# The linear recurrence unit of the odd layer, computed tile by tile beside that layer's input projection

## The chip, the core and the metric

The kernel runs on one core of a Trainium2 chip. The metric is the device time of one execution, in microseconds. Five engines of the core work on their own instruction streams and meet at semaphores: TensorE (PE in the profile; PEld is its weight load), VectorE (DVE), ScalarE (ACT), GpSimd (POOL) and SyncE (SP), which here only issues DMAs.

## What is computed

The reference is a model of two blocks; the first has attention and a mixture of experts, the second has an even and an odd layer. The change lies in the odd layer alone, whose mixer is (cut to what matters):

```
proj = h @ w_in                                  # 1024 tokens, 1024 -> 3072 columns
hq, hf, hi, hg, lx, lg = split(proj)             # six times 512 columns
hc = rms_norm(hgrn2(hq, hf, hi)) * silu(hg)
xc = conv_b + sum_j conv_w[j] * shift(lx, 3 - j) # causal convolution, 4 taps
r  = sigmoid(xc @ w_a + b_a)                     # blocks of 64 channels
ig = sigmoid(xc @ w_x + b_x)
a  = exp(-8 * r * softplus(-lam))
u  = sqrt(1 - a*a) * ig * xc                     # the factor is 1 at the first token
h_t = a_t * h_(t-1) + u_t                        # linear recurrence over the tokens
hl = h * silu(lg)
y  = concat(hc, hl) @ w_out
```

`hgrn2` is the other recurrence, in chunks of tokens and in four heads.

## The kernel before, in words

`second` builds the odd layer out of four stages. A stage (`stage`) owns its buffers and semaphores; at its end the semaphores are cleared and all engines meet at a barrier, so no work of one stage lies beside another's.

1. `project("pg", ...)`, lines 82 to 276, multiplies the normed activations `hT` (kept in SBUF as two parts, HI and LO) by the weights in six chunks of 512 columns. For each chunk SP loads 2 MB of weights into `raw` (two buffers, so the load of chunk g waits until chunk g-2 is split), ACT rounds them to the HI part (`split_hi`, line 193) and DVE forms the LO part (`split_lo`, line 204), eight instructions each. PE makes eight groups of 24 matmuls (`product`, line 78), each group into its own one of eight PSUM banks `acc`. ACT copies the even groups out (line 240), DVE the odd ones (line 276), and ACT issues the store of each group (line 242). ACT and DVE have the split of chunk g+1 in their streams ahead of the copies of chunk g, and `split_hi` of chunk g+1 waits for the last group of chunk g-1. The chunks come in the order q and f of `hgrn2` (stored transposed, `oT`), its value and gate (as rows, `orows`), and then the two of the linear recurrence unit: x and gate (transposed, rows 1024 to 2047 of `oT`). The scratch tensors lie in HBM.
2. `hgrn2`, lines 2416 to 2736, takes 8 units of 4 steps (`schedule`). In `prep` of a unit DVE forms differences of decays, ACT takes the exponentials (`hg_ex`, line 2559) and POOL multiplies (`hg_qk`, `hg_qb`, `hg_kb`, lines 2607 to 2616); `step(G)` is the PE work of one of 32 chunks of 128 tokens with its ACT copies (lines 2576 to 2586) and DVE sums. PE begins a unit once POOL has finished it. The parts of unit n+1's prep are interleaved with the steps of unit n.
3. `rg_lru`, lines 2742 to 2918, is the linear recurrence unit: four tiles of 128 channels by 1024 tokens. SP loads x and the gate of a tile from `oT`; DVE makes the convolution, four passes (2870 and 2873); PE the two gate products (2818); ACT the sigmoids (2827 to 2830), then for all tiles in turn the exponentials (2836), the hyperbolic tangents (2839) and the roots (2842); DVE the products and the scan (2903 to 2918); ACT and POOL write the two parts of the result into tiles 4 to 7 of `hT` (2845, 2805).
4. `mix_out("om", ...)` norms and gates the output of `hgrn2`, turns it into tiles 0 to 3 of `hT` and multiplies `hT` by `w_out` (line 726).

Of the kernel before, what the change touches and what calls it, by code (L numbers as in the profile page):

```python
# [14 lines left out]
P = 128  # L15
D = 1024
S = 1024
# [64 lines left out]
def project(nc, name, hT, nk, chunks, gain=None, also=None):  # L82
# [17 lines left out]
    uses = [[sum(groups(c) > j for c in chunks[:g]) for j in range(groups(ch))] for g, ch in enumerate(chunks)]  # L100
# [5 lines left out]
    kept = [[sum(groups(c) > j and "split" not in c for c in chunks[:g]) for j in range(NT)] for g in range(N + 1)]  # L106
    nst = [[16 * kept[g][j] for j in range(groups(ch))] for g, ch in enumerate(chunks)]
# [14 lines left out]
    with stage(nc) as st:  # L122
        raw = st.sb(name + "_raw", [P, 2, nk, BANK])
        w = st.sb(name + "_w", [P, 2, 2, nk, BANK], F32R)
        obuf = st.sb(name + "_o", [P, NT, BANK])
        cut = any("split" in ch for ch in chunks)
        parts = obuf[:, :, :].rearrange("p (x o a) n -> p x o a n", x=2, o=2).bitcast(F32R)
# [4 lines left out]
        acc = [st.ps(f"{name}_acc{j}", [P, BANK]) for j in range(NT)]  # L132
        gain_in = st.sem(name + "_gain_in")
        raw_in = [st.sem(f"{name}_raw_in{s}") for s in range(2)]
        k_in = [st.sem(f"{name}_k_in{k}") for k in range(nk)] if by_k else None
        hi_ok, lo_ok = st.sem(name + "_hi_ok"), st.sem(name + "_lo_ok")
        mm_done = [st.sem(f"{name}_mm{j}") for j in range(NT)]
        copied = [st.sem(f"{name}_copied{j}") for j in range(NT)]
        stored = [st.sem(f"{name}_stored{j}") for j in range(NT)]

        with nc.Block() as block:
            @block.sync
            def _(sp):
# [4 lines left out]
                for g, ch in enumerate(chunks):  # L148
                    if g >= 2:
                        sp.wait_ge(lo_ok, splits_to[g - 1])  # L150
# [5 lines left out]
                    for dst, src in ch["load"]:  # L156
                        sp.dma_start(raw[:, g % 2, 0:ks[g][1], dst], src).then_inc(raw_in[g % 2], 16)
                    if g == 1 and also:
                        also(sp)

            @block.tensor
            def _(pe):
                for g, ch in enumerate(chunks):
# [17 lines left out]

            def split_hi(act, g):

                n = chunks[g]["width"]
                if loads[g]:
                    act.wait_ge(raw_in[g % 2], 16 * sum(loads[g % 2:g + 1:2]))
# [2552 lines left out]

def rg_lru(nc, xT_in, A, hT):

# [239 lines left out]
```

## Time and profile before

| what | value |
|---|---|
| median of 3 runs | 2874.32 us (2871.42 to 2881.37) |
| the profiled execution's own time | 2867.56 us |
| its span in the trace | 2865.8 us |
| PE busy over the span | 2218.6 us (77%) |
| DVE, ACT, POOL busy | 1339.6, 1022.9, 535.9 us |
| first and last group of matmuls of the projection `pg` start | 2184.8 us, the last matmul 2448.6 us |

The span begins with the first instruction seen and ends with the last; positions below are microseconds from its start. The time of an execution is a little longer than its span. A stage's share is read by its stretch of positions.

### The profile page before, as it was taken

Reading aid. Unit: us, or ns where it says so; the run is one execution under the profiler, and the core shown is the slowest. Engines: PE = TensorE matmul, PEld = TensorE weight load, DVE = VectorE, ACT = ScalarE, POOL = GpSimd, SP = SyncE. Lnnn points to the kernel's source line nnn. Section 1 sums busy time; section 2 is a strip of 40 time slices with the busy share of each in tenths; the row PEclk is TensorE's granted clock in tenths of the full one; section 3 lists DMA queues with packets and bytes.
Section 4 is the critical chain, followed back from the end, with each engine's and each line's share of the span. In section 5 each row is a group of like instructions: output and inputs, shape, how many; then the busy total and the mean of one; then the engine's idle time right before and its main releaser. Section 6 shows DMA issues by size and latency. Waiting matters only on the chain. (4 is left out here: it accounts for less than half of the span.)

```text
span 2865.8 us, 34485 instructions
## 1 busy us (share of the span) xinstructions
PE 2218.6 (77%) x12244; PEld 1825.8 (64%) x12244; DVE 1339.6 (47%) x2217; ACT 1022.9 (36%) x1809; POOL 535.9 (19%) x630
## 2 busy tenths in 40 slices
PE   6996953999787599994399997688397999464248
PEld 5775942899775466663388885577386888354137
DVE  4223833655443666663612203677463211475753
ACT  4223732455331355552411100455242111463431
POOL 0000011522010121231200004334130000464122
PEclk7998976999888699997599998689698999677669
DMA  6647727522244399884533113321444311221043
GB/s 217 187 145 192 218 57 230 157 59 66 64 157 156 148 359 365 348 342 160 229 114 109 50 48 100 79 66 33 156 135 151 107 52 48 81 67 43 35 140 103
DMA packets 225569, 399.16 MB, mean 139 GB/s; under 512 B 99200, under 2 KB 121088, under 8 KB 212752
## 3 DMA queue, kind: packets, MB, share of 16 engines
q1 hardware_dynamic: 174912, 294.73, 32.5%
q10 hardware_dynamic: 40480, 83.64, 8.2%
q0 software_dynamic: 10032, 18.90, 1.7%
q8 instruction: 87, 1.43, 0.2%
q14 instruction: 58, 0.48, 0.1%
HBM read 300.16 MB, written 114.85 MB: 145 GB/s over the span
## 5 line engine op out<-in xcount | busy, mean ns | idle before, releaser
L78 PE MATMUL pe_acc<-pe_w,hT 128*128 128x512 f32 x960 | 219.7, 391 | 8.8 <-DVE pe_w L204 8.7
L78 PEld LDWEIGHTS pe_acc<-pe_w,hT 128*128 128x128 f32 x960 | 180.8, 189 | 47.6 <-DVE pe_w L204 10.0
L78 PE MATMUL ex_gu<-hT,ex_xT 128*128 128x512 f32 x792 | 194.4, 401 | 0.8 <-DVE hT L1966 0.8
L1966 DVE TENSOR_TENSOR hT<-ex_raw,hT 128x2048 fp32r<-128x2048 f32 x66 | 150.9, 2288 | 89.7 <-ACT hT L1937 86.2
L78 PE MATMUL pg_acc<-hT,pg_w 128*128 128x512 f32 x768 | 177.4, 393 | 8.6 <-DVE pg_w L204 8.6
L78 PEld LDWEIGHTS pg_acc<-hT,pg_w 128*128 128x128 f32 x768 | 146.0, 190 | 39.8 <-DVE pg_w L204 9.3
L78 PEld LDWEIGHTS ex_gu<-hT,ex_xT 128*128 128x128 f32 x792 | 147.5, 190 | 34.5 <-DVE hT L1966 1.2
L1937 ACT ACTIVATE hT<-ex_raw 128x2048 fp32r<-128x2048 f32 x66 | 126.1, 1912 | 43.2 <-PEq L47 23.9
L276 DVE COPY pe_o<-pe_acc 128x512 f32<-128x512 f32 x28 | 19.4, 692 | 238.5 <-PE pe_acc L78 238.5
L1255 PE MATMUL ab_op<-ab_v,ab_pT 128*128 128x64 f32 x1024 | 121.3, 272 | 0.0
L1895 PE MATMUL ex_dn<-ex_wd,ex_hT 128*128 128x512 f32 x264 | 118.7, 592 | 0.8 <-ACT ex_hT L1931 0.8
L1255 PEld LDWEIGHTS ab_op<-ab_v,ab_pT 128*128 128x128 f32 x1024 | 119.3, 192 | 0.0
L276 DVE COPY pg_o<-pg_acc 128x512 f32<-128x512 f32 x24 | 16.6, 691 | 205.0 <-PE pg_acc L78 205.0
L1266 DVE TENSOR_REDUCE ab_mx<-ab_s 128x1 f32<-128x1024 f32 x64 | 78.4, 1225 | 72.0 <-PE ab_s L1233 72.0
L2405 POOL TENSOR_TENSOR sb_w<-sb_be,sb_pr 128x128 f32<-128x128 f32 (+3 forms) x64 | 83.8, 1314 | 148.7 <-DVE sb_pr L2384 140.3
L78 PE MATMUL pa_acc<-hT,pa_w 128*128 128x512 f32 (+1 forms) x432 | 100.7, 395 | 8.7 <-DVE pa_w L204 8.7
L2707 PE MATMUL hg_s<-hg_qk 128*64 128x64 f32 x768 | 42.5, 262 | 82.3 <-POOL hg_kb L2616 82.3
L1230 PE MATMUL ab_s<-ab_kh,ab_qs 128*128 128x512 f32 x128 | 56.8, 444 | 54.8 <-DVE ab_krs L1287 54.3
L78 PEld LDWEIGHTS pa_acc<-hT,pa_w 128*128 128x128 f32 (+1 forms) x432 | 80.0, 185 | 29.0 <-DVE pa_w L204 9.1
L2384 DVE TENSOR_TENSOR_SCAN sb_pr<-sb_s,sb_ones 128x128 f32<-128x128 f32 (+3 forms) x64 | 86.5, 1351 | 20.5 <-ACT sb_s L2341 20.1
L2707 PEld LDWEIGHTS hg_s<-hg_qk 128*64 128x64 f32 x768 | 40.9, 173 | 84.4 <-issue 84.4
L240 ACT ACTIVATE pe_o<-pe_acc 128x512 f32<-128x512 f32 x28 | 16.6, 593 | 215.7 <-PE pe_acc L78 215.7
(455 smaller groups left out, 5195.6 us busy)
## 6 DMA issues: line engine op xcount, KB each, us to landing
ex_raw<-in_w_gate SPq DMA_DIRECT2D x33, 1024.0 KB, 7.4
ex_raw<-in_w_up SPq DMA_DIRECT2D x33, 1024.0 KB, 11.6
ex_wd<-in_w_down SPq DMA_DIRECT2D x33, 1024.0 KB, 13.8
pe_raw<-in_even_w_in SPq DMA_DIRECT2D x6, 2048.0 KB, 7.9
pg_raw<-in_odd_w_in SPq DMA_DIRECT2D x5, 2048.0 KB, 8.6
scr_q<-pa_o ACTq DMA_DIRECT2D x32, 256.0 KB, 3.9
scr_k<-pa_o ACTq DMA_DIRECT2D x32, 256.0 KB, 3.6
hT<-scr_k SPq DMA_DIRECT2D x16, 512.0 KB, 6.7
```

The lines of the kernel that those rows point to most:

```text
L78: mm = pe.matmul(out, a(p, k), b(q, k), start=(k == 0 and i == 0), stop=(k == n - 1 and i == 2))
L240: act.activation(obuf[0:m, j, 0:n], acc[j][0:m, 0:n], ACT.Copy).then_inc(copied[j], 1)
L276: dve.tensor_copy(obuf[0:m, j, 0:n], acc[j][0:m, 0:n]).then_inc(copied[j], 1)
L1230: pe.matmul(sps[l % 2][:, cc], qs[:, u, ii], kh[:, u, cc], start=True, stop=False)
L1255: mm = pe.matmul(ops[m % 2][:, 0:DV], pT[:, m % 2, k * P:(k + 1) * P], v[:, u, k, :], start=(k == 0), stop=(k == NT - 1))
L1266: dve.reduce_max(mx[:, l:l + 1], sps[l % 2][:, :], AX.X).then_inc(max_done, 1)
L1895: mm = pe.matmul(dn[:, n * BANK:(n + 1) * BANK], hTs[:, b % 2, k, :], wd[:, b % ND, k * D + n * BANK:k * D + (n + 1) * BANK], start=(k == ...
L1937: act.activation(split(s, HI)[:, :, g, :], raw[:, s % NW, g, :].rearrange("p (k n) -> p k n", k=8), ACT.Copy).then_inc(w_hi, 1)
L1966: dve.tensor_tensor(split(s, LO)[:, :, g, :], raw[:, s % NW, g, :].rearrange("p (k n) -> p k n", k=8), split(s, HI)[:, :, g, :].bitcast(F3 ...
L2384: dve.tensor_tensor_scan(pr[:, l % 2, S - n:S][:, ::-1], sps[l % 2][:, 0:n][:, ::-1], ones[:, 0:n], 1.0, ALU.mult, ALU.mult).then_inc(pr_o ...
L2405: pool.tensor_tensor(w[:, l % 4, 0:n], be[:, l % 4, 0:n], pr[:, l % 2, S - n + 1:S + 1], ALU.mult).then_inc(w_ok, 1)
L2707: pe.matmul(sps[G % 2][b0:b0 + HB, (l - 1) * HB:l * HB], qk[:, n % 2, l, half], qk[:, n % 2, l, half], start=True, stop=True, skip_group_c ...
```

## The change

The stage `rg_lru` goes. Its work is now in a class `Lru`, whose methods are called from inside `project` at fixed places of each engine's stream: tile t is worked on while PE makes chunk t+1. The projection's chunks are put in another order, x and gate of the unit first. `project` gets three arguments: `ring`, the number of PSUM banks and output buffers, taken in turn over all chunks (6 here in place of 8, since the unit needs two banks), `nraw`, the number of weight buffers (1 here in place of 2), and `beside`. The result of the unit goes to a scratch tensor `lrT`; `hgrn2` loads it in one DMA of 2 MB, and splits it there into the two parts in `hT`: ACT one tile in each of steps 12 to 15, POOL all four at its end. The other calls of `project` keep 8 and 2 and have chunks of 8 groups (the last chunk of one has 2), so that their banks are taken as before.

The loop over `chunks` with `sp` is SP's stream, `beside.tensor` stands behind each group of PE, `beside.scalar` behind each store issued by ACT, `beside.vector` behind each (possible) copy of DVE; POOL multiplies the gate by its sigmoid in a stream of its own. In `hgrn2`, `lru.load` is in SP's stream, `lru.hi` in ACT's `step`, `lru.lo` in POOL's stream behind `schedule`. In `Lru.scalar` each step waits for what it reads, and `j` 2 also for the product with the gate of the tile before (`hg_ok`). The diff, cut to its core (`slot(g, j)` stands for `j` wherever a bank, buffer or semaphore is named, and `g % nraw` for `g % 2` with `raw`):

```diff
-def project(nc, name, hT, nk, chunks, gain=None, also=None):
+def project(nc, name, hT, nk, chunks, gain=None, also=None, ring=NT, nraw=2, beside=None):
+    base = [sum(groups(c) for c in chunks[:g]) for g in range(N + 1)]
+    slot = lambda g, j: (base[g] + j) % ring
+    uses = [[(base[g] + j) // ring for j in range(groups(ch))] for g, ch in enumerate(chunks)]
...
+        def landed(eng, g, j):
+            eng.wait_ge(stored[slot(g, j)], nst[g][j] + 16)
+        beside = beside(st, landed) if beside else None
...
                 for g, ch in enumerate(chunks):
-                    if g >= 2:
-                        sp.wait_ge(lo_ok, splits_to[g - 1])
+                    if beside and g >= 2:
+                        beside.sync(sp, g - 2)
+                    if g >= nraw:
+                        sp.wait_ge(lo_ok, splits_to[g - nraw + 1])
...
+                if beside:
+                    for g in range(N - 2, N):
+                        beside.sync(sp, g)
+                    beside.sync_end(sp)
...
                         mm.then_inc(mm_done[u], 1)
+                        if beside:
+                            beside.tensor(pe, g, j)
...
                         act.dma_start(dst(j), obuf[0:m, u, 0:n]).then_inc(stored[u], 16)
+                        if beside:
+                            beside.scalar(act, g, j)
...
                             dve.tensor_copy(obuf[0:m, u, 0:n], acc[u][0:m, 0:n]).then_inc(copied[u], 1)
+                        if beside:
+                            beside.vector(dve, g, j)
...
-def rg_lru(nc, xT_in, A, hT):
...
+class Lru:
+    NTI = 4
...
+    def load_x(self, sp, t):
+        self.landed(sp, 0, 2 * t)
+        self.landed(sp, 0, 2 * t + 1)
+        if t >= 2:
+            sp.wait_ge(self.conv, 4 * (t - 1))
+        sp.dma_start(self.x[:, t % 2, 4:S + 4], self.src[t * P:(t + 1) * P, :]).then_inc(self.x_in[t % 2], 16)
+    def load_gate(self, sp, t):
+        self.landed(sp, 1, 2 * t)
+        self.landed(sp, 1, 2 * t + 1)
+        if t >= 1:
+            sp.wait_ge(self.gs_ok, t)
+        sp.dma_start(self.gt[:, :], self.src[512 + t * P:512 + (t + 1) * P, :]).then_inc(self.g_in, 16)
+    def store(self, sp, t):
+        sp.wait_ge(self.hg_ok, t + 1)
+        sp.dma_start(self.out[t * P:(t + 1) * P, :], self.o[:, :]).then_inc(self.kept, 16)
+    def sync(self, sp, g):
+        if g == 0:
...
+            self.load_x(sp, 0)
+            self.load_x(sp, 1)
+        elif g == 1:
+            self.load_gate(sp, 0)
+            self.load_x(sp, 2)
+        elif g <= self.NTI + 1:
+            if g + 1 < self.NTI:
+                self.load_x(sp, g + 1)
+            if g - 1 < self.NTI:
+                self.load_gate(sp, g - 1)
+            self.store(sp, g - 2)
...
+    def tensor(self, pe, g, j):
+        t = g - 1
+        if not (0 <= t < self.NTI and j in (2, 3)):
+            return
+        h = j - 2
...
+        pe.wait_ge(self.conv, 4 * (t + 1))
+        if t or h:
+            pe.wait_ge(self.r_ok, 2 * t + h)
+            pe.wait_ge(self.ig_ok, 2 * t + h)
+        nn = slice(h * BANK, (h + 1) * BANK)
+        pe.matmul(self.pa[:, :], self.wa[:, t, :], self.xc[:, nn], start=True, stop=True)
+        pe.matmul(self.px[:, :], self.wx[:, t, :], self.xc[:, nn], start=True, stop=True).then_inc(self.mm, 1)
+    def scalar(self, act, g, j):
...
+        if j in (2, 3):
...
+            act.activation(self.r[:, nn], self.pa[:, :], ACT.Sigmoid, bias=self.ba[:, t:t + 1]).then_inc(self.r_ok, 1)
+            act.activation(self.ig[:, nn], self.px[:, :], ACT.Sigmoid, bias=self.bx[:, t:t + 1]).then_inc(self.ig_ok, 1)
+        elif j == 4:
...
+            act.activation(self.sg[:, :], self.gt[:, :], ACT.Sigmoid).then_inc(self.sg_ok, 1)
...
+            act.activation(self.a[:, :], self.r[:, :], ACT.Exp, scale=self.sm[12][:, t:t + 1]).then_inc(self.a_ok, 1)
...
+            act.activation(self.xc[:, :], self.r[:, :], ACT.Tanh, scale=self.sm[11][:, t:t + 1]).then_inc(self.th_ok, 1)
+        elif j == 6:
...
+            act.activation(self.xc[:, :], self.xc[:, :], ACT.Sqrt).then_inc(self.mu_ok, 1)
...
+    def vector(self, dve, g, j):
...
+        if j == 0:
...
+            dve.tensor_scalar(cv, src[0], self.cw[:, t, 0:1], self.cb[:, t:t + 1], ALU.mult, ALU.add).then_inc(self.conv, 1)
+            for i, (o, z) in enumerate(((xc, cv), (cv, xc), (xc, cv)), 1):
...
+        elif j == 4:
+            dve.wait_ge(self.ig_ok, 2 * (t + 1))
...
+        elif j == 5:
+            dve.wait_ge(self.a_ok, t + 1)
+            step(dve.tensor_tensor(cv, self.a[:, :], self.a[:, :], ALU.mult))
+            dve.wait_ge(self.th_ok, t + 1)
...
+        elif j == 6:
+            dve.wait_ge(self.mu_ok, t + 1)
...
+            step(dve.memset(self.xc[:, 0:1], 1.0))
+            step(dve.tensor_tensor(cv, xc, self.ig[:, :], ALU.mult))
+            step(dve.tensor_tensor_scan(self.r[:, :], self.a[:, :], cv, 0.0, ALU.mult, ALU.add))
+        elif j == 7:
+            dve.wait_ge(self.gs_ok, t + 1)
+            if t >= 1:
+                dve.wait_ge(self.kept, 16 * t)
+            dve.tensor_tensor(self.o[:, :], self.r[:, :], self.sg[:, :], ALU.mult).then_inc(self.hg_ok, 1)
...
+class LruParts:
+    def load(self, sp):
+        sp.dma_start(self.hT[:, LO, 4:8, :].bitcast(F32), self.src.rearrange("(t p) s -> p t s", p=P)).then_inc(self.raw_in, 16)
+    def hi(self, act, t):
+        act.wait_ge(self.raw_in, 16)
+        act.activation(self.hT[:, HI, 4 + t, :], self.hT[:, LO, 4 + t, :].bitcast(F32), ACT.Copy).then_inc(self.hi_ok, 1)
+    def lo(self, pool, t):
+        pool.wait_ge(self.hi_ok, t + 1)
+        pool.tensor_tensor(self.hT[:, LO, 4 + t, :], self.hT[:, LO, 4 + t, :].bitcast(F32), self.hT[:, HI, 4 + t, :].bitcast(F32),
+                           ALU.subtract).then_inc(self.lo_ok, 1)
...
                 load_qv(1)
+                lru.load(sp)
...
                         act.activation(ob[:, h % 2, c, :], ops[:, 0:P], ACT.Copy).then_inc(ob_ok, 1)
+                    if 12 <= G < 16:
+                        lru.hi(act, G - 12)
...
                 schedule(lambda G: None, prep)
+                for t in range(4):
+                    lru.lo(pool, t)
...
-    project(nc, "pg", hT, 8, [T_chunk(wo, c, scr["oT"], c) for c in (0, 512)] +
-            [row_chunk(wo, 1024 + c, scr["orows"], c) for c in (0, 512)] +
-            [T_chunk(wo, 2048 + c, scr["oT"], 1024 + c) for c in (0, 512)], gain=[(0, A["pre_norm_w_2"][1])])
-    hgrn2(nc, ident, scr["oT"], scr["orows"], C, scr["hc"])
-    rg_lru(nc, scr["oT"][1024:2048, :], A, hT)
+    project(nc, "pg", hT, 8, [T_chunk(wo, 2048 + c, scr["oT"], 1024 + c) for c in (0, 512)] +
+            [T_chunk(wo, c, scr["oT"], c) for c in (0, 512)] +
+            [row_chunk(wo, 1024 + c, scr["orows"], c) for c in (0, 512)], gain=[(0, A["pre_norm_w_2"][1])], ring=6, nraw=1,
+            beside=lambda st, landed: Lru(nc, st, A, scr["oT"][1024:2048, :], scr["lrT"], landed))
+    hgrn2(nc, ident, scr["oT"], scr["orows"], C, scr["hc"], lambda st: LruParts(st, scr["lrT"], hT))
```

## Rows read from the trace of the kernel before

**Rows 1.** Busy time by stage; columns stand in the first line.
```profile
core 0: us, PE busy (x) PEld busy (x) DVE busy (x) ACT busy (x) POOL busy (x), PEclk, DMA share, GB/s
...
2184.00:2452.00 268.00, 264.23 (x1152) 218.06 (x1152) 49.15 (x72) 43.58 (x71) 0.00 (x0) 0.99 0.25 92
2452.00:2638.00 186.00, 92.58 (x1312) 81.26 (x1312) 117.52 (x261) 100.52 (x207) 106.84 (x131) 0.72 0.21 59
2638.00:2737.00 99.00, 21.21 (x32) 8.10 (x32) 68.59 (x70) 33.19 (x32) 20.81 (x10) 0.60 0.16 45
...
2765.00:2866.00 101.00, 91.64 (x411) 75.45 (x410) 37.38 (x59) 22.54 (x77) 23.73 (x46) 0.96 0.31 99
```

**Rows 2.** Timeline, start us and duration us: end of the recurrence stage.
```profile
2638.20 0.53 POOL L2796 MEMSET lr_wa<- 128x512 f32 x1 [17.17 <-POOLq L47]
...
2733.95 2.34 POOL L2805 TENSOR_TENSOR hT<-lr_hg,hT 128x1024 fp32r<-128x1024 f32 x1 [4.57 <-ACT hT L2845]
2737.17 0.32 SPq L405 DMA_DIRECT2D omf_x<-scr_hc  x1
```

**Rows 3.** Timeline of DVE in the projection, first chunks.
```profile
2220.58 0.69 DVE L276 COPY pg_o<-pg_acc 128x512 f32<-128x512 f32 x1 [10.19 <-PE pg_acc L78]
2231.46 0.69 DVE L276 COPY pg_o<-pg_acc 128x512 f32<-128x512 f32 x1 [10.19 <-PE pg_acc L78]
2233.44 5.39 DVE L204 SCALAR_TENSOR_TENSOR pg_w<-pg_raw,pg_g,pg_w 128x512 fp32r<-128x512 f32 x8 [1.29 <-ACT pg_w L193]
```

**Rows 4.** Timeline of ACT in the projection, beginning of chunk 1.
```profile
2232.62 5.02 ACT L193 ACTIVATE pg_w<-pg_raw,pg_g 128x512 fp32r<-128x512 f32 x8 [6.00 <-DVE pg_o L276]
```

**Rows 5.** Timeline of PE and DVE in the linear recurrence stage.
```profile
2648.03 3.32 DVE L2873 SCALAR_TENSOR_TENSOR lr_xc<-lr_x,lr_cw,lr_cv 128x1024 f32<-128x1024 f32 x1
...
2654.14 3.75 PE L2818 MATMUL lr_pa<-lr_xc,lr_wa 128*128 128x512 f32 x4 [20.88 <-DVE lr_xc L2873]
...
2662.21 1.95 PE L2818 MATMUL lr_pa<-lr_xc,lr_wa 128*128 128x512 f32 x4 [2.26 <-ACT lr_ig L2830]
...
2664.00 1.88 PE L2818 MATMUL lr_px<-lr_xc,lr_wx 128*128 128x512 f32 x4
...
2673.30 0.80 DVE L2870 TENSOR_SCALAR lr_cv<-lr_x,lr_cw,lr_cb 128x1024 f32<-128x1024 f32 x1
...
2676.78 1.28 DVE L2873 SCALAR_TENSOR_TENSOR lr_xc<-lr_x,lr_cw,lr_cv 128x1024 f32<-128x1024 f32 x1
...
2686.30 1.28 ACT L2832 ACT_TABLE_LOAD   x1
2687.59 0.20 ACT L2832 ACTIVATE lr_sm<-lr_sm 128x4 f32<-128x4 f32 x1
...
2708.49 2.29 DVE L2914 TENSOR_TENSOR_SCAN lr_hs<-lr_a,lr_u 128x1024 f32<-128x1024 f32 x1
```

**Rows 6.** Groups of the linear recurrence stage: count, busy us, mean ns, idle before.
```profile
L2805 POOL TENSOR_TENSOR hT<-lr_hg,hT 128x1024 fp32r<-128x1024 f32 x4 | 9.4, 2340 | 44.8 <-ACT hT L2845 44.8
...
L2829 ACT ACTIVATE lr_r<-lr_pa,lr_ba 128x1024 f32<-128x1024 f32 x4 | 4.5, 1115 | 27.1 <-PE lr_px L2818 27.1
...
L2842 ACT ACTIVATE lr_xc<-lr_xc 128x1024 f32<-128x1024 f32 x4 | 4.1, 1053 | 1.7 <-DVE lr_xc L2905 1.5
```

**Rows 7.** DMA issues, KB each and us to landing.
```profile
pg_raw<-in_odd_w_in SPq DMA_DIRECT2D x5, 2048.0 KB, 8.6
```

**Rows 8.** Timeline of ACT in the other recurrence.
```profile
2456.64 1.06 ACT L2535 ACTIVATE hg_k<-hg_f 128x1024 f32<-128x1024 f32 x1 [12.42 <-DMA hg_f<-scr_oT]
...
2549.03 0.28 ACT L2586 ACTIVATE hg_ob<-hg_o 128x128 f32<-128x128 f32 x1 [1.63 <-PE hg_o L2736]
...
2552.59 1.29 ACT L2559 ACTIVATE hg_ex<-hg_df 128x512 f32<-128x512 f32 x2 [1.01 <-DVE hg_df L2653]
```

**Rows 9.** Timeline of POOL at the end of the other recurrence.
```profile
2619.77 1.26 POOL L2616 TENSOR_TENSOR hg_kb<-hg_k,hg_el 128x512 f32<-128x512 f32 x1
```

**Rows 10.** The chain that ended last: start us, duration us.
```profile
2765.64 11.94 PE om_acc L726 x48
```

More of the change, by code:

```diff
@@ L104, in project @@
         loads[0] = 0
-    kept = [[sum(groups(c) > j and "split" not in c for c in chunks[:g]) for j in range(NT)] for g in range(N + 1)]
-    nst = [[16 * kept[g][j] for j in range(groups(ch))] for g, ch in enumerate(chunks)]
+    plain = [(base[g] + j) % ring for g, ch in enumerate(chunks) for j in range(groups(ch)) if "split" not in ch]
+    first = sum(groups(ch) for ch in chunks if "split" in ch)
+    nst = [[16 * plain[:max(0, base[g] + j - first)].count(slot(g, j)) for j in range(groups(ch))] for g, ch in enumerate(chunks)]
     def outs(x):
@@ L185, in split_hi @@
                 if loads[g]:
[L186 removed]
+                    act.wait_ge(raw_in[g % nraw], 16 * sum(loads[g % nraw:g + 1:nraw]))
                 if g >= 2:
                     last = groups(chunks[g - 2]) - 1
[L189 removed]
+                    act.wait_ge(mm_done[slot(g - 2, last)], uses[g - 2][last] + 1)
                 for k in range(ks[g][1]):
@@ L198, in split_lo @@
                 if loads[g]:
-                    dve.wait_ge(raw_in[g % 2], 16 * sum(loads[g % 2:g + 1:2]))
+                    dve.wait_ge(raw_in[g % nraw], 16 * sum(loads[g % nraw:g + 1:nraw]))
                 for k in range(ks[g][1]):
@@ L2413, with hgrn2 @@
 LEVELS = [64, 32, 16, 8, 4, 2, 1]
-def hgrn2(nc, ident, fT_in, v_in, C, out):
+def hgrn2(nc, ident, fT_in, v_in, C, out, beside):
     NL = len(LEVELS)
@@ new lines, in __init__ @@
+    def __init__(self, nc, st, A, src, out, landed):
+        self.A, self.src, self.out, self.landed = A, src, out, landed
+        n4 = self.NTI
+        sb = lambda n, *shape: st.sb("lr_" + n, [P, *shape])
+        self.x, self.gt = sb("x", 2, S + 4), sb("gt", S)
+        self.cv, self.xc, self.r, self.ig, self.a, self.sg, self.o = (sb(n, S) for n in ("cv", "xc", "r", "ig", "a", "sg", "o"))
+        self.wa, self.wx = sb("wa", n4, P), sb("wx", n4, P)
+        self.cw, self.cb = sb("cw", n4, 4), sb("cb", n4)
+        self.ba, self.bx, self.lam = sb("ba", n4), sb("bx", n4), sb("lam", n4)
+        self.sm = [sb(f"sm{i}", n4) for i in range(13)]
+        self.pa, self.px = st.ps("lr_pa", [P, BANK]), st.ps("lr_px", [P, BANK])
+        (self.consts_in, self.cleared, self.e_ok, self.d, self.conv, self.mm, self.r_ok, self.ig_ok, self.u1_ok, self.c8_ok, self.a_ok,
+         self.th_ok, self.m2_ok, self.mu_ok, self.sg_ok, self.gs_ok, self.pads, self.wab_in, self.hg_ok, self.g_in, self.kept) = (
+            st.sem("lr_" + n) for n in ("consts", "cleared", "e_ok", "step", "conv", "mm", "r_ok", "ig_ok", "u1_ok", "c8_ok", "a_ok", "th_ok",
+                                        "m2_ok", "mu_ok", "sg_ok", "gs_ok", "pads", "wab_in", "hg_ok", "g_in", "kept"))
+        self.x_in = [st.sem(f"lr_x_in{u}") for u in range(2)]
+        self.steps = 0
```

314 lines of the change are left out of this document (125 added, 189 removed).

## The prediction, made before the changed kernel was run

> **What bounds the kernel now.** I read the odd layer stage by stage, because a barrier stands at the end of each stage and nothing of one can hide another's work. The table of windows [rows 1] shows four regimes. In the projection PE is busy for 264.23 of 268 us at a granted clock of 0.99, while DVE and ACT work 49 and 44 us: PE alone sets its length, and the other engines have some 200 us free. In the other recurrence no engine is full; it goes by a chain through DVE, ACT and POOL. In the stage of the linear recurrence unit (2638 to 2737) DVE works 68.6 of 99 us, PE 21, and everything hangs on that stage's own chain. The last stretch belongs to PE again, with the matmuls of the output product on the chain that ended last [rows 10].
>
> So the reader is to see a stage of 99 us whose DVE work (69 us) and ACT work (33 us) would fit into the free time of the stage two places ahead of it. Whether it fits in time too, chunk by chunk, is the question.
>
> **What goes.** The first instruction of the unit's stage starts at 2638.20, the first of the next stage at 2737.17 [rows 2]. Between equal barriers that is 2737.17 - 2638.20 = 98.97 us, all of it serial. The next stage begins with weight loads and norms that need nothing from the removed one but tiles 4 to 7 of `hT`, so it starts that much earlier and otherwise as before: **-99.0**.
>
> **What PE gets in the projection.** One tile costs PE eight matmul records (four products of 512 columns, each run as two). At the full clock they took from 2662.21 to 2664.00 + 1.88 = 2665.88, so 3.67 us [rows 5]; four tiles make 14.7 us. These stand in PE's stream between groups and nothing hides them: **+14.7**. At half the clock the two products with `lr_pa` alone took 3.75 us [rows 5], so a tile would be some 7.5 us and four of them 30. I take the full clock, since the rows of the projection have 0.99.
>
> **Do they wait there?** A group of 24 matmuls takes half of 2231.46 - 2220.58 [rows 3], so 5.44 us; a chunk with a tile beside it takes 8 x 5.44 + 3.67 = 47.2. Call the start of a chunk zero.
> - The convolution. ACT's split of the next chunk starts 1.2 after zero (2232.62 against 2231.46) and takes 5.02 [rows 4]; DVE's ends at 2233.44 + 5.39 = 2238.83, so 7.4 after zero [rows 3]. Then come four passes, from 2673.30 to 2676.78 + 1.28, or 4.76 [rows 5]: ready at 12.2. PE wants it behind its third group, at 16.3. Slack 4.1.
> - The second half's products wait until ACT has read the first half's banks. PE ends those at 16.3 + 1.84 = 18.1; ACT loads a table (1.28, [rows 5]) and makes two sigmoids of half of 1115 ns [rows 6], rounded up to 0.6 each: 20.6. PE comes there at 18.1 + 5.44 = 23.6. Slack 3.0.
> - The end of a tile runs into the next chunk. Group 7 (the seventh made) is out at 3.67 + 7 x 5.44 = 41.8; ACT's copy, table load and root (0.6 + 1.28 + 1.05 and an issue of some 0.3) give 45.0; DVE's product (1.28, as a pass of the convolution) and scan (2.29 [rows 5]) give 48.6, its copy of the last group 49.3, its last product 50.6. That copy was out at 0.7 after zero, now at 2.1, and ACT's next split waits behind it: DVE's split ends at about 8.8 and the convolution at 13.6. Slack against 16.3 still 2.7.
> - The copies. With six banks PE comes back to a bank after six groups, 33 us; the latest copy above is not 10 us late. Eight banks or six make no difference.
> - The weights. One buffer instead of two: the load of a chunk now waits for the split one chunk ahead, and on SP it also stands behind `beside.sync`. The latest case is the one behind `store`, which waits for the product at 3.4 of the next chunk; behind the wait for the convolution it is 13.6. The 2 MB then take 8.6 us to land, median [rows 7], so 22 after zero, and are wanted at 47. Slack 25. In chunk 0 the second load is issued when the first split is done, some 7 us later than now, while PE has six empty banks before it.
> - Gate, x and store of a tile: each waits for something at most one chunk old and is wanted half a chunk later or more.
>
> Bounds of this part: nothing on top of 14.7, or, if one of the slacks of 3 to 4 us is gone by a few microseconds, some waits (below). DVE ops that meet POOL's product can lose 2.0 (3.32 against 1.28 [rows 5]); POOL's falls at about 33 to 35, when DVE has time. ACT's table loads are three per tile in place of three in all; in the chain just given they are counted, and elsewhere ACT is idle. I take **0**.
>
> Of those loads the Trainium skill says more ("ScalarE: Activation LUTs", What ACT_TABLE_LOAD costs): 1283 ns for the load and some 1380 ns to drain, 2.66 us a switch. In the trace the instruction behind the load starts 2687.59 - 2686.30 = 1.29 us after it [rows 5], and ACT was just done with a sigmoid when it began. By the page's figure the sigmoids are ready at 22.0 in place of 20.6, still ahead of 23.6; the sum would be the same here, and 1.4 us more in the step below.
>
> **What the other recurrence gets.** At its start ACT's first sigmoid follows its DMA wait with no load, at 2456.64 [rows 8], since the table from before fits. Now the last table of the projection is the root's, so a load of 1.28 stands ahead of it, on the chain that lets PE start: **+1.3**. Between nothing (if it is done during the 12.42 us of waiting) and 1.3 I take the latter.
>
> ACT's four rounding copies, 1.05 us each (as the other 128x1024 activations, [rows 6]), fall into steps 12 to 15, the unit that follows 2544. In step 12 ACT goes from `hg_ob` at 2549.03 straight to the exponentials [rows 8], and POOL waits for them: a full 1.05. In the next step ACT had 1.01 us idle before its exponentials [rows 8], so it hides the copy or not, as DVE was itself shifted; the third is like it and the fourth stands before a longer wait. From 1.0 (one of four shows) to 4.2 (all), I take two: **+2.0**. POOL's four parts stand behind its last `hg_kb`, which ends at 2619.77 + 1.26 = 2621.03 [rows 9]. Four of 2.34 [rows 6] end at 2630.4; the stage lasts till the next at 2638.2, so they hide with over 5 us to spare. If that cover were gone they cost up to 9.4. The 2 MB load is issued behind the first two heads' loads and has some 85 us before step 12; the later heads' loads go behind it and are wanted later still: 0.
>
> **Sum.** -99.0 + 14.7 + 0 + 1.3 + 2.0 = -81.0. The profiled execution took 2867.56, so 2786.6 by its own time. The median of the runs shown is 2874.32, 6.8 above that execution; against it the forecast is **2793 us**.
>
> **Rivals.**
> 1. *PE waits at the unit's products, and its clock falls.* For it: the slacks are 2.7 to 4.1 us over chains of a dozen instructions on two engines with in-order streams. Against: each step above has a row. If each of the eight places cost a wait of 1 to 2 us, that is 8 to 16. Before such a wait in the unit's own stage PE came back at the low level: 3.75 us where 1.95 is usual [rows 5], so 1.8 lost per pair of products, and as much again for the matmuls behind. Eight times 1 to 4.5 is 8 to 36; with 81 as the base the time is 2801 to 2829. The Trainium skill has the rule ("TensorE: Matmul & The Clock Gate", Part 1: The HAM clock gate): the default is the throttled clock, and only activity releases it. By it these waits would matter only if PE were long idle; the rows at 0.60 in the unit's stage against 0.99 in the projection [rows 1] agree.
> 2. *Slower than before: the weight load behind `store` on SP.* One weight buffer and one queue: if the store's wait for a tile's last product comes late, the load is late, the split is late, PE stands, and so does the next tile. To cost more than it brings it must eat the slack of 25 and then 81 / 4 = 20 more in each of four chunks, so the tile's last product would have to come about 45 us after the next chunk begins, not 3. Nothing in the rows is near this. Time above 2874.
> 3. *The work in the other recurrence shows in full:* 1.3 + 4.2 + 9.4 = 14.9 in place of 3.3, 2805 us. For it: that stage is one chain through three engines. Against: POOL's free tail of 17 us before 2638.20 [rows 2, 9].
> 4. *A little better than forecast:* neither table load nor copies show, and the first chunk's weights land sooner without the second's beside them: 3 to 5 us less, 2789.
>
> **Chances.** Forecast (2786 to 2799) 0.66; rival 1, 0.16; rival 3, 0.08; rival 4 below 2786, 0.04; stalls between them up to 2870, 0.03; rival 2, 0.03. The range 2784 to 2812 holds the forecast, nearly all of rivals 3 and 4, and the mild half of rival 1, and leaves out 0.15 or so. A measurement of this kernel tells no less than 0.3% (8.6 us) from no change; only rival 2 ends at or above that: faster 0.96, same 0.01, slower 0.03.
>
> **What would show it.** The projection should last some 283 us in place of 268, with PE busy nearly throughout, clock near 1.0, 32 new matmul records of about 0.45 us, and no idle time before them put down to DVE's convolution or ACT's `lr_ig`. ACT's first sigmoid in the other recurrence should have a table load ahead of it; that stage should last 189 to 190 us. The next stage should start at about 2656 and be unchanged. I am wrong if idle time of several microseconds stands before `lr_pa` in every chunk, if `pg_raw` lands after ACT wants it, or if POOL's `hT` in the other recurrence ends last there.

## The result, and the profile after

The changed kernel takes 2775.9 us, median of 4 runs (2772.64 to 2779.28), beside 2872.87 for the kernel before in the same series: ratio 0.9663, 95% interval 0.9631 to 0.9694. That is faster, as forecast, but the time lies below the range of 2784 to 2812. The two profiled executions differ by less than the medians: 2867.56 - 2779.28 = 88.3 us, against 97.0. So there are two questions: why the traces differ by 88 where the sum said 81, and where the other 9 come from.

The windows of the changed kernel, answering to [rows 1] (projection, other recurrence, output product; same columns):

```profile
core 0: us, PE busy (x) PEld busy (x) DVE busy (x) ACT busy (x) POOL busy (x), PEclk, DMA share, GB/s
2185.00:2466.00 281.00, 277.09 (x1184) 223.49 (x1184) 103.73 (x142) 87.31 (x117) 9.59 (x4) 0.99 0.31 110
2466.00:2649.00 183.00, 89.86 (x1312) 78.69 (x1312) 117.31 (x261) 104.98 (x212) 115.94 (x135) 0.72 0.25 71
2676.00:2777.00 101.00, 92.53 (x412) 76.19 (x411) 37.35 (x59) 22.53 (x77) 23.66 (x46) 0.96 0.29 99
```

The projection still is PE's: 277.09 busy of 281 us at a clock of 0.99, now with 1184 matmul records for 1152. DVE and ACT have twice their former work in it. The next timeline is PE's in that stage of the changed kernel: start, duration, instruction.

```profile
2229.70 17.39 PE L78 MATMUL pg_acc<-hT,pg_w 128*128 128x512 f32 x76
2246.92 1.02 PE L2867 MATMUL lr_pa<-lr_xc,lr_wa 128*128 128x512 f32 x2
2247.78 1.02 PE L2868 MATMUL lr_px<-lr_xc,lr_wx 128*128 128x512 f32 x2
2248.24 6.05 PE L78 MATMUL pg_acc<-hT,pg_w 128*128 128x512 f32 x24
2254.12 1.02 PE L2867 MATMUL lr_pa<-lr_xc,lr_wa 128*128 128x512 f32 x2
2254.98 1.02 PE L2868 MATMUL lr_px<-lr_xc,lr_wx 128*128 128x512 f32 x2
2255.43 38.69 PE L78 MATMUL pg_acc<-hT,pg_w 128*128 128x512 f32 x168
2293.96 1.02 PE L2867 MATMUL lr_pa<-lr_xc,lr_wa 128*128 128x512 f32 x2
```

Nothing stands in brackets behind the unit's products, here or in the rest of the stage: PE never waits for them. From 2246.92 to 2293.96 a chunk with its tile takes 47.04 us; 8 groups of 5.44 are 43.52, so a tile costs 3.52, where I had 3.67. DVE's convolution in the second of these chunks:

```profile
2286.77 0.81 DVE L2938 TENSOR_SCALAR lr_cv<-lr_x,lr_cw,lr_cb 128x1024 f32<-128x1024 f32 x1
...
2290.25 1.28 DVE L2941 SCALAR_TENSOR_TENSOR lr_xc<-lr_x,lr_cw,lr_cv 128x1024 f32<-128x1024 f32 x1
```

It is ready at 2291.53, which is 2.43 us ahead of PE's 2293.96; my estimate of that slack was 2.7. The weight loads on SP (start, duration):

```profile
2213.05 0.43 SPq L168 DMA_DIRECT2D pg_raw<-in_odd_w_in  x1
...
2246.42 0.42 SPq L168 DMA_DIRECT2D pg_raw<-in_odd_w_in  x1
...
2292.97 0.48 SPq L168 DMA_DIRECT2D pg_raw<-in_odd_w_in  x1
...
2333.92 0.38 SPq L168 DMA_DIRECT2D pg_raw<-in_odd_w_in  x1
```

The last three are issued 16, 15 and 9 us after PE began a chunk (2230.8, 2277.8, 2324.9), and what they load is wanted at that chunk's end.

The other recurrence begins with ACT's table load and first sigmoid, and contains the four copies in ACT's steps 12 to 15 (two of them here) and POOL's four parts at its end:

```profile
2466.50 1.28 ACT L2566 ACT_TABLE_LOAD   x1 [8.86 <-PEq L47]
2470.07 1.06 ACT L2566 ACTIVATE hg_k<-hg_f 128x1024 f32<-128x1024 f32 x1 [2.28 <-DMA hg_f<-scr_oT]
```

```profile
2561.14 0.28 ACT L2617 ACTIVATE hg_ob<-hg_o 128x128 f32<-128x128 f32 x1 [1.50 <-PE hg_o L2771]
2561.32 1.05 ACT L2978 ACTIVATE hT<-hT 128x1024 fp32r<-128x1024 f32 x1
2562.26 1.14 ACT L2590 ACTIVATE hg_ex<-hg_df 128x512 f32<-128x512 f32 x2
...
2563.72 1.05 ACT L2978 ACTIVATE hT<-hT 128x1024 fp32r<-128x1024 f32 x1
2564.67 0.63 ACT L2590 ACTIVATE hg_ex<-hg_df 128x512 f32<-128x512 f32 x1
```

```profile
2562.96 0.73 POOL L2640 TENSOR_TENSOR hg_qk<-hg_k,hg_ex 128x256 f32<-128x256 f32 x1 [4.70 <-ACT hg_ex L2590]
...
2564.34 0.74 POOL L2640 TENSOR_TENSOR hg_qk<-hg_k,hg_ex 128x256 f32<-128x256 f32 x1
...
2565.72 0.73 POOL L2640 TENSOR_TENSOR hg_qk<-hg_k,hg_ex 128x256 f32<-128x256 f32 x1
...
2567.09 0.75 POOL L2640 TENSOR_TENSOR hg_qk<-hg_k,hg_ex 128x256 f32<-128x256 f32 x1
...
2631.45 1.26 POOL L2649 TENSOR_TENSOR hg_kb<-hg_k,hg_el 128x512 f32<-128x512 f32 x1
2632.67 9.34 POOL L2982 TENSOR_TENSOR hT<-hT 128x1024 fp32r<-128x1024 f32 x4
```

The table load starts with the stage, not behind the wait for the first DMA, as I had assumed; the sigmoid waits 2.28 us more for its data after it. In the kernel before, POOL waited three times in this unit:

```profile
2549.95 0.73 POOL L2607 TENSOR_TENSOR hg_qk<-hg_k,hg_ex 128x256 f32<-128x256 f32 x1 [3.95 <-ACT hg_ex L2559]
...
2553.30 0.73 POOL L2607 TENSOR_TENSOR hg_qk<-hg_k,hg_ex 128x256 f32<-128x256 f32 x1 [0.54 <-ACT hg_ex L2559]
...
2556.39 0.85 POOL L2607 TENSOR_TENSOR hg_qk<-hg_k,hg_ex 128x256 f32<-128x256 f32 x1 [0.29 <-ACT hg_ex L2559]
```

Now the first wait is 4.70 us and the two later ones of 0.54 and 0.29 are gone: POOL works through without a gap once it has started. POOL's four parts end at 2642.01, ahead of the stage's end at 2649.56.

### The profile page after: what moved, and what is told of

It is laid out like the page before. It is cut to its first block and busy times, and to the rows that moved or that the text cites. A ratio compares the mean times of both kernels' runs of the same rounds, so it can differ in the third digit from the quotient of the medians.

```text
span 2777.3 us, 34500 instructions
## 1 busy us (share of the span) xinstructions
PE 2217.5 (80%) x12244; PEld 1832.4 (66%) x12244; DVE 1325.1 (48%) x2217; ACT 1037.8 (37%) x1828; POOL 540.0 (19%) x630
## 5 line engine op out<-in xcount | busy, mean ns | idle before, releaser
L2742 PEld LDWEIGHTS hg_s<-hg_qk 128*64 128x64 f32 x768 | 39.1, 168 | 84.9 <-issue 84.9
L2348 PE MATMUL sb_op<-sb_v,sb_wT 128*128 128x64 f32 x576 | 84.5, 299 | 10.5 <-PE sb_t L2330 5.9
```

The lines of the kernel that those rows point to most:

```text
L2348: mm = pe.matmul(ops[m % 2][:, 0:DV], wT[:, m % 2, k * P:(k + 1) * P], v[:, u, k, :], start=(k == 0), stop=(k == i))
L2742: pe.matmul(sps[G % 2][b0:b0 + HB, (l - 1) * HB:l * HB], qk[:, n % 2, l, half], qk[:, n % 2, l, half], start=True, stop=True, skip_group_c ...
```

## The experiments

All stage lengths below are differences between the first SP instructions of successive stages, one profiled execution per kernel; "last" is from there to the end of the span. The starts were read to 0.1 us, so a length can be off by as much. Experiments 1 to 4 ran on one chip, 5 to 8 on a second and 9 to 11 on a third.

| kernel | projection starts | projection | other recurrence | unit | last |
|---|---|---|---|---|---|
| before | 2179.6 | 273.3 | 185.5 | 98.8 | 128.6 |
| before_again | 2179.9 | 272.3 | 184.0 | 97.9 | 128.4 |
| order_only | 2178.1 | 273.1 | 184.9 | 99.0 | 128.1 |
| after | 2180.2 | 286.3 | 183.1 | - | 127.7 |
| after_again | 2176.2 | 287.8 | 184.1 | - | 128.3 |
| no_parts | 2176.9 | 287.3 | 184.1 | - | 127.2 |
| table_back | 2180.0 | 287.6 | 184.3 | - | 128.3 |
| pe_double | 2190.6 | 300.1 | 185.3 | - | 128.1 |
| conv_late4 | 2177.2 | 303.0 | 185.6 | - | 127.6 |
| conv_late8 | 2180.7 | 326.3 | 183.5 | - | 128.6 |
| parts_last | 2191.6 | 287.6 | 190.6 | - | 127.7 |
| copies_double | 2185.8 | 286.4 | 186.2 | - | 127.7 |
| copies_step12 | 2196.4 | 287.6 | 187.3 | - | 127.6 |

The second column is the same code in every kernel, and it moves over 20 us. Whole times of single executions therefore tell little about an edit of a few microseconds; the stage lengths do.

**1. The changed kernel again, `after_again`.** No edit, five executions.

> The changed kernel once more, timed in five rounds. By my steps it gains what the two profiled executions differ by, 2867.56 - 2779.28 = 88 us (ratio 0.969); the medians shown so far differ by 97 (ratio 0.966). If the gap of 9 is the spread of single executions, this run gives a gain of 86 to 94; if the change brings something that no step of mine has, it stays at 97 or more.

2778.35 us (2774.78 to 2780.92) against 2865.83 (23 runs, 2861.0 to 2878.46): ratio 0.9696, interval 0.9681 to 0.971, so 87.1 us. The gain is what the traces show. Of the 9.9 us by which the first series gave more, 7.0 lie in its kernel before, whose four runs had a median that much above that of these 23, and 2.5 in the changed kernel. Whether that is the chance of four executions or something that lasted through the series is not shown.

**2. The kernel before against itself, `before_again`.** No edit.

> The kernel before against itself. It prices the spread of executions: I expect a ratio of 1.000 within 0.003, single executions up to 8 us from their median, and a second trace of the other recurrence (stage starts 2452.94 and 2638.20, so 185.3 us) that differs by 1 to 2 us with no edit at all. If it repeats within 0.3 us, the 2.2 us that this stage became shorter belong to the change.

2870.91 us (2859.92 to 2890.58), ratio 1.0018, interval 1.0 to 1.0036. Single executions lie up to 20 us from the median, more than I expected, and even medians of 12 and of 23 executions of one kernel differ by 5.1 us. The other recurrence took 184.0 us in place of 185.5 with no edit, so most of the 2 us by which it is shorter in the trace of the changed kernel need not come from the change.

**3. Order and buffers alone, `order_only`.** The kernel before with the new arguments; the unit stays a stage:

```diff
-    project(nc, "pg", hT, 8, [T_chunk(wo, c, scr["oT"], c) for c in (0, 512)] + ...
+    project(nc, "pg", hT, 8, [T_chunk(wo, 2048 + c, scr["oT"], 1024 + c) for c in (0, 512)] +
+            [T_chunk(wo, c, scr["oT"], c) for c in (0, 512)] +
+            [row_chunk(wo, 1024 + c, scr["orows"], c) for c in (0, 512)], gain=[(0, A["pre_norm_w_2"][1])], ring=6, nraw=1)
```

> The kernel before with the new chunk order, six banks and one weight buffer; the unit remains a stage of its own. My theory: no change in time (ratio 0.997 to 1.003), only the first chunk of the projection about 1 us shorter, since its weights have the queues to themselves. The rival, that the new order or buffers bring a part of the surplus over my forecast, says 5 to 10 us faster.

2866.57 us, ratio 1.0001, interval 0.9985 to 1.0016; projection 273.1 us, between the 272.3 and 273.3 of the unedited kernels. One weight buffer, six banks and the order cost nothing and bring nothing that shows (the interval leaves room for some 4 us either way); the microsecond that I expected in the first chunk does not show beyond the spread.

**4. Nothing in the other recurrence, `no_parts`.** `lru.load`, `lru.hi` and `lru.lo` are not called, so tiles 4 to 7 of `hT` are without the unit's result:

```diff
-                lru.load(sp)
...
-                    if 12 <= G < 16:
-                        lru.hi(act, G - 12)
...
-                for t in range(4):
-                    lru.lo(pool, t)
```

> The changed kernel without the 2 MB load, ACT's four copies and POOL's four parts in the other recurrence (tiles 4 to 7 of the activations are then not the unit's result, so this part of the computation is left out). My forecast had priced them at 2.0 us; the trace says that they are hidden. By the forecast this kernel is 2 us faster than the changed one, by the new reading the same (within 1 us in the length of that stage, 183.1 us in the changed kernel).

The stage takes 184.1 us, exactly as in `after_again`; 2779.15 us (2774.9 to 2789.26) beside 2778.35. The load, the copies and the parts cost nothing that shows.

**5. The products doubled, `pe_double`.**

```diff
+        pe.matmul(self.pa[:, :], self.wa[:, t, :], self.xc[:, nn], start=True, stop=True)
+        pe.matmul(self.px[:, :], self.wx[:, t, :], self.xc[:, nn], start=True, stop=True)
         pe.matmul(self.pa[:, :], self.wa[:, t, :], self.xc[:, nn], start=True, stop=True)
         pe.matmul(self.px[:, :], self.wx[:, t, :], self.xc[:, nn], start=True, stop=True).then_inc(self.mm, 1)
```

> Each of the 16 products of the unit is issued twice in the projection. If PE alone sets the length of that stage, this adds the price of the products once more: 4 x 3.5 = 14 us by the changed kernel's trace (14.7 by my forecast), ratio to before 0.974. If PE has idle time beside the products that could take them, less than 10 us.

PE's timeline of this kernel:

```profile
2257.51 1.02 PE L2867 MATMUL lr_pa<-lr_xc,lr_wa 128*128 128x512 f32 x2
...
2307.96 1.02 PE L2867 MATMUL lr_pa<-lr_xc,lr_wa 128*128 128x512 f32 x2
```

A chunk with a tile now takes 50.45 us, 3.41 more; the projection is 300.1 us, 12.9 more than the 287.2 that seven kernels average whose projection has no edit that PE meets (`after`, `after_again`, `no_parts`, `table_back` and those of experiments 9 to 11; 286.3 to 287.8). PE's time is the price of this stage, at full rate. The whole time, 2802.6 us (2779.87 to 2813.06), is too scattered to say more.

**6 and 7. A late convolution, `conv_late4` and `conv_late8`.** Idle passes on DVE ahead of each tile's convolution, 4 and 8:

```diff
             src = [self.x[:, u, 1 + i:1 + i + S] for i in range(4)]
+            for _ in range(4):
+                step(dve.scalar_tensor_tensor(out=cv, in0=src[0], scalar=self.cw[:, t, 0:1], in1=src[1], op0=ALU.mult, op1=ALU.add))
```

> Four idle passes on DVE ahead of each tile's convolution, 5.2 us more each. The trace of the changed kernel has the convolution ready 4.05 us ahead of PE in the first tile and 2.43 in the others, so PE should wait 1.2 and three times 2.8, about 9.5 us in all, with idle time put down to DVE's convolution. If the clock falls after such waits (my first rival), the cost is 15 us or more; if PE has more slack than I read, under 5.

> Eight idle passes per tile, 10.5 us more each: waits of 6.4 and three times 8.1, so 31 us if waits alone count. If TensorE comes back from them at its low clock, some us more for each, 40 us or more, and the granted clock of the projection's chunks below 0.99.

PE with four passes (first tile, second tile, beginning of the third), and with eight (beginning of the second tile, then the third). In brackets stands PE's idle time and who ended it:

```profile
2246.64 1.10 PE L2867 MATMUL lr_pa<-lr_xc,lr_wa 128*128 128x512 f32 x2 [1.22 <-DVE lr_xc L2943]
...
2248.04 6.05 PE L78 MATMUL pg_acc<-hT,pg_w 128*128 128x512 f32 x24
...
2296.69 1.44 PE L2867 MATMUL lr_pa<-lr_xc,lr_wa 128*128 128x512 f32 x2 [2.76 <-DVE lr_xc L2943]
2297.91 1.92 PE L2868 MATMUL lr_px<-lr_xc,lr_wx 128*128 128x512 f32 x2
2298.84 6.94 PE L78 MATMUL pg_acc<-hT,pg_w 128*128 128x512 f32 x24
...
2348.37 1.92 PE L2867 MATMUL lr_pa<-lr_xc,lr_wa 128*128 128x512 f32 x2 [2.76 <-DVE lr_xc L2943]
```

```profile
2310.83 2.07 PE L2867 MATMUL lr_pa<-lr_xc,lr_wa 128*128 128x512 f32 x2 [8.03 <-DVE lr_xc L2943]
...
2368.28 2.07 PE L2867 MATMUL lr_pa<-lr_xc,lr_wa 128*128 128x512 f32 x2 [8.03 <-DVE lr_xc L2943]
2370.14 1.92 PE L2868 MATMUL lr_px<-lr_xc,lr_wx 128*128 128x512 f32 x2
2371.07 7.05 PE L78 MATMUL pg_acc<-hT,pg_w 128*128 128x512 f32 x24
```

The waits are as I read them from the changed kernel: 1.22 and three times 2.76 (9.5 us in all); 6.50, 8.03, 8.03 and 8.04 (30.6). But the projection became 303.0 - 287.2 = 15.8 and 326.3 - 287.2 = 39.1 us longer. The rest, 6.3 and 8.5 us, goes with a low clock: after the wait of 1.22 the pair of products takes its usual 1.02 us or little more, after 2.76 it takes 1.44 and 1.92, after 8.03 it takes 2.07 and 1.92, and the group behind takes 6.94 and 7.05 in place of 6.05. The granted clock (third column from the right) by stretch, with eight passes and then in the changed kernel:

```profile
2274.00:2329.00 55.00, 46.97 (x191) 36.41 (x190) 31.21 (x31) 15.58 (x22) 0.73 (x1) 0.91 0.29 101
```

```profile
2274.00:2321.00 47.00, 47.00 (x201) 37.55 (x200) 20.93 (x23) 17.95 (x24) 2.40 (x1) 1.00 0.37 134
```

By the stage lengths each of these waits costs itself and some 2.1 us of low clock (6.3 / 3 and 8.5 / 4). The traces give it one by one, as what a chunk takes beyond its 47.04 us and its wait: 51.68 from 2296.69 to 2348.37 is 1.9 more than 47.04 + 2.76, and 57.45 from 2310.83 to 2368.28 is 2.4 more than 47.04 + 8.03. The next chunk of each has 2.0 and 2.6, the one behind the wait of 6.50 has 1.8, and the one behind the wait of 1.22 only 0.25. So the price of the clock is about 2 us a wait, but for the shortest, and the waits of 8.03 cost 0.4 to 0.8 us more than those of 2.76.

The whole times are 2795.63 us (2795.04 to 2800.78; ratio 0.9775) and 2820.09 (2816.18 to 2840.22; ratio 0.9872, interval 0.983 to 0.9915). Eight idle passes a tile, 10.5 us of DVE, take back about half of what the change brings.

**8. The table load taken out of the other recurrence, `table_back`.**

```diff
+        if g == 5 and j == 0:
+            act.activation(self.sm[1][:, :], self.sm[1][:, :], ACT.Sigmoid)
```

> One tiny sigmoid of 128x4 on ACT in the last chunk of the projection, so that the table of the other recurrence's first sigmoid is loaded by then. My forecast had the load on the path there (1.3 us); by the trace it lies in the wait for the first DMA, so this saves nothing: POOL's first product comes 15.3 us after the stage begins either way. By the forecast it would come at 14.0.

ACT at the beginning of that stage:

```profile
2471.19 1.06 ACT L2566 ACTIVATE hg_k<-hg_f 128x1024 f32<-128x1024 f32 x1 [12.43 <-DMA hg_f<-scr_oT]
```

No load ahead of the sigmoid any more, which comes 3.6 us after the stage begins (2467.6), as in the changed kernel (2470.07 against 2466.5). POOL's first product comes 15.3 us after the stage begins in both. The load had cost nothing. The whole time, 2783.89 us (2782.16 to 2793.87; ratio 0.974), is 5.5 above that of `after_again`, but from the projection's start on its stages are as long within 0.2 us; in its trace the code ahead of the projection ends 3.9 us later, so the whole time says nothing of this edit.

**9. No cover for the parts, `parts_last`.** ACT's copies stand behind all steps, POOL's parts behind them:

```diff
-                    if 12 <= G < 16:
-                        lru.hi(act, G - 12)
...
                 schedule(step, prep)
+                for t in range(4):
+                    lru.hi(act, t)
```

> ACT's four copies of the unit's result moved behind all steps of the other recurrence, and POOL's four parts with them. Now nothing covers them: after the last output copy (2645.0 in the changed kernel) come one copy of 1.05 and four parts of 2.34, ending at about 2655.7, in place of a stage end at 2649.6 with some 1 us of barrier. So this stage is 7 us longer (190 to 191 us) and ratio to before about 0.972. If a gap between POOL's parts appears, up to 9. If the parts cost nothing even here, the same as the changed kernel.

The end of that stage on POOL:

```profile
2644.79 1.26 POOL L2649 TENSOR_TENSOR hg_kb<-hg_k,hg_el 128x512 f32<-128x512 f32 x1
2659.62 9.24 POOL L2982 TENSOR_TENSOR hT<-hT 128x1024 fp32r<-128x1024 f32 x4 [13.56 <-ACT hT L2978]
2669.83 0.10 POOL L444 MEMSET omf_half<- 128x1 f32 x1 [0.97 <-POOLq L47]
```

From PE's start of the last unit (2646.16) to the next stage it takes 23.7 us, in the changed kernel 16.7 (2632.82 to 2649.56): 6.9 more, and the stage 190.6. The cover that I named was real, and its absence costs what the durations say. The whole time is 2793.85 us (ratio 0.9758, interval 0.9716 to 0.98).

**10 and 11. How much ACT work the unit of steps 12 to 15 absorbs, `copies_double` and `copies_step12`.** In the first each copy is made twice; in the second all four stand in step 12:

```diff
     def hi(self, act, t):
         act.wait_ge(self.raw_in, 16)
+        act.activation(self.hT[:, HI, 4 + t, :], self.hT[:, LO, 4 + t, :].bitcast(F32), ACT.Copy).then_inc(self.again, 1)
+        act.wait_ge(self.again, t + 1)
```

```diff
-                    if 12 <= G < 16:
-                        lru.hi(act, G - 12)
+                    if G == 12:
+                        for t in range(4):
+                            lru.hi(act, t)
```

> Each of ACT's four copies in steps 12 to 15 is done twice, so 4.2 us more on ACT in that unit. In the changed kernel the unit with the copies took 17.73 us from PE's start to the next (17.90 before), so one copy a step is fully absorbed. The absorption has an end: gaps of POOL before its products were 0.54 and 0.29 there. I expect the unit to become 1 to 4 us longer; if it stays at 17.7, ACT has more room in it than the gaps say.

> All four copies in step 12 at once, in front of the exponentials for which POOL waits: 3.2 us more there than one copy. My forecast took each copy in front of the exponentials as a delay of the chain. If so the unit is about 3 us longer, 20.5 to 21. If POOL catches up later in the unit, less than 1.5.

From PE's start of that unit to that of the next:

| kernel | ACT copies in it | unit, us |
|---|---|---|
| before | none | 17.90 |
| before_again | none | 17.74 |
| no_parts | none | 17.80 |
| after | one a step | 17.73 |
| after_again | one a step | 17.87 |
| copies_double | two a step | 19.99 |
| copies_step12 | four in step 12 | 20.68 |

One copy a step vanishes; a second costs 2.2 of the 4.2 us that it takes; four at once cost 2.9. The whole times of two executions each, 2784.35 and 2789.01 us, scatter too much to say anything of this. POOL with two a step, and then the head of the unit with four in step 12:

```profile
2569.93 0.73 POOL L2640 TENSOR_TENSOR hg_qk<-hg_k,hg_ex 128x256 f32<-128x256 f32 x1 [5.48 <-ACT hg_ex L2590]
...
2573.43 0.73 POOL L2640 TENSOR_TENSOR hg_qk<-hg_k,hg_ex 128x256 f32<-128x256 f32 x1 [0.69 <-ACT hg_ex L2590]
...
2576.93 0.84 POOL L2640 TENSOR_TENSOR hg_qk<-hg_k,hg_ex 128x256 f32<-128x256 f32 x1 [0.70 <-ACT hg_ex L2590]
```

```profile
2583.99 0.73 POOL L2641 TENSOR_TENSOR hg_qk<-hg_k,hg_ex 128x256 f32<-128x256 f32 x1 [7.67 <-ACT hg_ex L2590]
```

With two a step it waits in every part, 0.69 and 0.70 us, and the wait at the unit's head has grown to 5.48 from 4.70 with one copy. With four in step 12 it waits once, 7.67 us. POOL's waits explain the unit's length in all four kernels: together they are 4.78 us before (3.95 + 0.54 + 0.29), 4.70 with one copy a step, 6.87 with two and 7.67 with four at once, and the unit takes 17.90, 17.73, 19.99 and 20.68. What POOL can catch up is its two later waits, 0.83 us; the 0.75 that one copy adds at the head just fits into them.

## Why the prediction was right and where it was wrong

The time fell below the stated range. Of the sum, the two large terms held; the steps that failed are three smaller ones, all upward: +1.3 for the table load and +2.0 for ACT's copies, which measured 0 each, and the 6.8 added to pass from the profiled execution to the median of three.

- *The stage goes, -99.0.* Right: 98.8, 97.9 and 99.0 in three traces that have it.
- *PE's products at the full clock, +14.7.* Right. The projection is 287.2 us in seven traces and 272.9 in three without the unit, +14.3; a tile costs 3.52.
- *Nothing waits, 0.* Right, step by step: convolution ready 4.04 us ahead in the first tile (I had 4.1) and 2.43 in the later ones (2.7), the first half's last sigmoid done at 2250.67, 3.45 ahead of PE's 2254.12 (3.0), weights early, banks free. The slack is real and narrow: experiments 6 and 7 used it up and got the waits of its size. The first rival was right that the clock would fall, but its price for that (1.8 us a pair and as much behind, so 3.6) was above the measured 2 or so, and it charged it to waits of 1 to 2 us, where the wait of 1.22 cost nothing of the kind. Its own numbers do not add up either: a wait of 2 with 3.6 behind it is 5.6, not 4.5, so its upper end should have been 45 us and not 36. It did not happen, since nothing was late. The Trainium skill's rule ("TensorE: Matmul & The Clock Gate", Part 1: The HAM clock gate), that the clock has to be earned by activity, agrees with experiments 6 and 7. What I made of it, that such waits matter only if PE is long idle, does not: 2.76 us was enough.
- *The table load, +1.3.* Wrong: 0. I had taken it to stand behind the DMA wait; it runs before it. I had named this end of the bound and chosen the other. On its length, the Trainium skill's load plus drain ("ScalarE: Activation LUTs", What ACT_TABLE_LOAD costs) would be 2.66 us. Here the sigmoid waited for its data, so no drain can be read off; 2.66 too would have been hidden, since 3.6 pass before the data are in. Where ACT waits for nothing, in the projection of the changed kernel, the measurement differs from that figure:

```profile
2262.52 1.06 ACT L2887 ACTIVATE lr_sg<-lr_gt 128x1024 f32<-128x1024 f32 x1 [0.40 <-ACT pg_o L259]
2263.60 1.28 ACT L2890 ACT_TABLE_LOAD   x1
2264.89 1.15 ACT L2890 ACTIVATE lr_a<-lr_r,lr_sm 128x1024 f32<-128x1024 f32 x1
```

The sigmoid ends at 2263.58 and the exponential starts at 2264.89, 1.31 us later, with a load of 1.28 between them. The load's length agrees with the Trainium skill's; its drain of 1.38 us has no room here.
- *ACT's copies, +2.0.* Wrong: 0. The first copy does delay the exponentials for which POOL waits (its wait is 4.70 in place of 3.95), but POOL then works without its later gaps, and the unit ends when it did. The room is only 0.83 us (experiments 10 and 11), so that the cost is 0 and not part of a microsecond is in part luck. I looked for what a copy delays next, and not for what the delayed engine can catch up by the end of the unit.
- *POOL's parts and the load, 0.* Right (experiment 4, which also rules out the third rival); experiment 9 shows the 7 us that they cost without cover.
- *The sum against the median.* This is the largest single part of the miss. With the two wrong terms at 0 the sum is -84.3, and 2867.56 - 84.3 = 2783.3 by the profiled execution's own time; the stage lengths of experiments 1 to 3 and of the first two traces average 556.3 before (three traces, order_only among them) and 470.7 after for the part from the projection's start to the last stage, 85.6 less. To that forecast I had added 6.8, because the median of three runs was 6.8 above the profiled execution. With 23 runs the median was 2865.83, 1.7 *below* it, and with the 12 of experiment 2 added, 2867.09, 0.5 below: the profiled execution was an ordinary one, and the three shown were high. 2865.83 - 84.3 = 2781.5 is within 3.2 us of the 2778.35 measured in the same series. The whole distance from the unrounded forecast of 2793.4 to the 2775.9 of the first series is 17.5 us: 6.8 for the offset, 3.3 for the two terms, 4.0 by which the changed kernel's profiled execution (2779.28) lies below 2783.3, and 3.4 from there to its median. The last two are of the size by which executions of one kernel differ.
- *The range.* Its lower end of 2784 left no room for the low ends that the text itself had named (0 for load and copies), nor for the spread of three runs. Low ends and own time give 2867.56 - 99.0 + 14.7 = 2783.3, and the spread of medians (5.1 us in experiment 2) asks for some 5 less. The fourth rival (a little better than forecast, load and copies hidden) is what happened, but not through the first chunk's weights. I had given it too little, and only for its part below 2786; its own 2789 lay inside the forecast.

What the remaining 3 us of the second series are is not settled. In `after` and `after_again` the other recurrence and the last stage are 1.2 and 0.4 us shorter than in the three traces without the change; over all six kernels that have the changed kernel's recurrence (183.1 to 185.6) it is only 0.5. No experiment ties this to the change. Nor is it settled why the code ahead of the projection, the same in every kernel, takes up to 20 us longer in some traces. That scatter is in every whole time: against the kernel before on its own chip `table_back`, whose stages are those of the changed kernel, gains 79.3 us, `after_again` 87.1, the first series 97.0.

No version here beats the changed kernel.

## What to carry to other kernels

A serial stage whose engines differ from those that bound an earlier stage is worth almost its whole length there, less the work of the bound engine. Price that work at full rate, list the slack of each handover into the bound engine's stream, and keep each positive, since a wait there costs its own length and, for those of 2.76 to 8 us here, about 2 us of low clock more. Where work is added to a helper engine in a pipelined unit, follow the delay to the unit's end before charging it; and add no offset between one execution and a median of three.

## What was not expected of the hardware

- Executions of one kernel on one chip ranged from 2859.92 to 2890.58 us, with no edit, and identical code ahead of the projection ended anywhere from 2176.2 to 2196.4.
- A PE wait of 1.22 us left the clock of the following products as it was (1.10 and 1.02 us for the pairs), one of 2.76 did not (up to 1.92 each), and one of 8.03 cost only 0.4 to 0.8 us more low clock than one of 2.76.
- Between two activations of different tables with nothing to wait for stood the load of 1.28 us and no more (2263.58 to 2264.89).
- The table load in front of an activation did not wait for what the activation waited for, at a stage's start: it began at 2466.50 with the stage, the activation at 2470.07. In the unit's stage of the kernel before, whose first activation has two waits ahead of it (constants and gate), the load began at 2643.44 with the gate's landing and the activation at 2646.79 with the constants'. That one wait stays behind the load and the others ahead of it is my reading of these two places; it was not tried.
